# Second pass of a two-block kernel: order of two norms, roots per tile, a projection in two halves, later row fills

## The reference

```python
# end of the first block
h = h + peer(rmsnorm(h, g_ffn[i]), w_q[i], sub_keys[i], expert_u[i], expert_v[i])
gate = jax.nn.sigmoid(rmsnorm(h, g_ple[i]) @ w_pg[i])     # norm n1, product pg
h = h + (p[i] @ w_pe[i]) * gate                           # product e
x = rmsnorm(h, g_final)                                   # norm f
# second block
h = rmsnorm_2(x, g_mix[l])                                # norm n2
proj = h @ w_in[l]                                        # product in2
mixed = concatenate([rmsnorm_2(sb, g_sb_out), rmsnorm_2(pooled, g_pool_out)])
x = x + mixed @ w_out[l]                                  # product o2
x = x + memory_cross_attention(rmsnorm_2(x, g_mem_q), rmsnorm_2(mem, g_mem_kv), ...)   # norm n3, products mq and mo
x = x + moe_ffn(rmsnorm_2(x, g_ffn), ...)                 # norm n4, router, experts
```

## Time and profile before

| | us |
|---|---|
| median of 3 runs | 3245.73 |
| lowest and highest | 3245.32, 3246.43 |
| run of the profiled execution | 3242.78 |
| its span | 3240.9 |
| TensorE busy in the span | 2547.0 (79%) |
| VectorE busy | 1372.6 (42%) |
| ScalarE busy | 682.0 (21%) |
| GpSimd busy | 721.0 (22%) |

### The profile page before, as it was taken

How to read it: one execution, slowest core, us unless ns; L and a number is a source line. 1 busy time by engine, 2 the same in 40 slices (tenths; PEclk the granted TensorE clock), 3 DMA queues, 4 the chain that set the end, 5 groups by cost and what they waited for, 6 DMA issues and landing times. The chain is left out here.

```text
span 3240.9 us, 33257 instructions
## 1 busy us (share of the span) xinstructions
PE 2547.0 (79%) x12781; PEld 1193.5 (37%) x12781; DVE 1372.6 (42%) x3005; ACT 682.0 (21%) x1902; POOL 721.0 (22%) x632
## 2 busy tenths in 40 slices
PE   6987887576556858667687687959999999999994
PEld 3435332242111414322345576723333333333331
DVE  1935667666778686565543123151111111101013
ACT  1112233222223232353231143110000000000001
POOL 0201344334445433644330010200000000000002
PEclk9998998797687979888998899979999999999997
DMA  4217999999999999999996621259999999999997
GB/s 164 78 46 294 407 401 386 372 404 421 421 417 416 418 392 415 378 415 421 421 421 254 194 88 52 69 232 420 406 387 405 412 404 406 413 408 415 404 412 282
DMA packets 152529, 1099.44 MB, mean 339 GB/s; under 512 B 17744, under 2 KB 24400, under 8 KB 54608
## 3 DMA queue, kind: packets, MB, share of 16 engines
q0 software_dynamic: 79232, 556.31, 42.3%
q1 hardware_dynamic: 64848, 529.97, 41.2%
q10 hardware_dynamic: 8288, 11.02, 1.0%
HBM read 1065.77 MB, written 31.46 MB: 339 GB/s over the span
## 5 line engine op out<-in xcount | busy, mean ns | idle before, releaser
L1912 PE MATMUL banks<-arena,spare 128*64 128x512 f32 x2048 | 635.1, 753 | 429.2 <-ACT spare L1853 423.6
L1783 DVE SCALAR_TENSOR_TENSOR arena<-arena 128x1024 f32<-128x1024 f32 x512 | 626.2, 1225 | 446.9 <-DMA arena<-in_expert_uv,picked 446.0
L1674 POOL DMA_INDIRECT arena<-in_expert_uv,picked x512 | 590.2, 1153 | 917.3 <-PE banks L1912 689.0
L2159 PE MATMUL banks<-arena,aT 128*64 128x512 f32 (+1 forms) x4032 | 609.3, 502 | 21.0 <-DMA arena<-in_expert_w 16.1
L1912 PEld LDWEIGHTS banks<-arena,spare 128*64 128x64 f32 x2048 | 147.4, 160 | 836.6 <-ACT spare L1853 607.4
L2159 PEld LDWEIGHTS banks<-arena,aT 128*64 128x64 f32 (+1 forms) x4032 | 208.9, 125 | 395.9 <-issue 341.8
L2171 PE MATMUL banks<-arena,aT 128*64 128x512 f32 (+1 forms) x2016 | 310.8, 509 | 8.9 <-ACT aT L2280 8.7
L2474 DVE TENSOR_SCALAR aT<-banks 128x512 f32<-128x512 f32 (+1 forms) x49 | 30.1, 615 | 632.6 <-PE banks L2177 632.6
L2099 POOL DMA_INDIRECT picked<-moe_rows,extra x32 | 30.5, 954 | 1004.4 <-PE banks L2145 951.7
L1842 ACT ACTIVATE spare<-spare 128x2 f32<-128x2 f32 x256 | 52.0, 203 | 902.3 <-DVE arena L1783 902.0
L1108 PE MATMUL banks<-arena,aT 128*128 128x256 f32 x768 | 179.6, 392 | 1.5 <-DVE aT L1075 0.8
(11 more groups left out here) (303 smaller groups left out, 2096.7 us busy)
## 6 DMA issues: line engine op xcount, KB each, us to landing
arena<-in_expert_w SPq DMA_DIRECT2D x192, 2048.0 KB, 31.9
arena<-in_mid_w SPq DMA_DIRECT2D x58, 1024.0 KB, 9.0
arena<-in_w_q SPq DMA_DIRECT2D x8, 2048.0 KB, 13.9
expert_rows<-aT ACTq DMA_DIRECT2D x70, 128.0 KB, 8.8
arena<-in_expert_uv,picked POOLq DMA_INDIRECT x512, 12.5
expert_rows<-h SPq DMA_DIRECT2D x8, 1024.0 KB, 12.1
arena<-in_w_in SPq DMA_DIRECT2D x3, 2048.0 KB, 19.0
arena<-in_w_out SPq DMA_DIRECT2D x2, 2048.0 KB, 8.2
```

Of the source, the lines that this page charges most:

```text
L1674: eng.indirect_dma_start(places[place_of[n]], None, uv_rows, bass.IndirectOffsetOnAxis(ap=eidx[:, n:n + 1], axis=0))\
L1783: nc.vector.scalar_tensor_tensor(out=u, in0=u, scalar=1.0, in1=twice[tt % 2][:, n % 2, :], op0=ALU.mult, op1=ALU.mult, accum_out=dots[:, k ...
L1912: mm = nc.tensor.matmul(bank[g * HALF:(g + 1) * HALF, sum_bank[tt] + half, :], diag[:, (n + g) % NDIAG, :], places[place_of[n + g]][:, D + ...
L2159: mm = nc.tensor.matmul(bank[tile, b_, 0:width], xT[:, c % 2 * 4 + k, r0:r0 + nrows], w[:, k * D + lo:k * D + lo + width], start=c % 2 == ...
```

## The change

- The first norm of pass two (n1) stands ahead of "mo" of pass one on ScalarE and VectorE, its transposes directly behind "mo" on TensorE. n1 of pass two has row tiles of its own (`rows1[1]`, at region 4096). n4 of pass one stands behind n1's copies on VectorE and its transposes behind pg on TensorE. The wait for the stored rows moves to f's squares.
- In pass two every norm takes root, reciprocal and scaled row one tile after the other.
- In pass two o2 goes over the pooled channels of all four units first (four banks are held), then forms "ssum", then goes over the attention channels.
- The row fills hang on unit ("o2", 1, 3), the router's loads on ("mq", 1, 3).

```diff
             else:
+                pel += [("mo", 0, u) for u in range(4)] + turned_labels("n1", 1) + [("pg", 1, u) for u in range(4)] + turned_labels("n4", 0)
+                acl += squared_labels("n1", 1) + squared_labels("n4", 0)
+                dvl += scaled_labels("n1", 1) + [("mo", 0, u) for u in range(4)] + turned_labels("n1o", 1)
+                dvl += scaled_labels("n4", 0) + turned_labels("n4o", 0)
...
+                if s:
+                    eng.wait_ge(*when("act", (name + "q", s, i)))
+                    nc.scalar.activation(stat[:, c + 2 + i:c + 3 + i], stat[:, c + i:c + i + 1], ACT.Sqrt, scale=1.0 / D,
+                                         bias=const("eps", eps_col, eps_col + 1)).then_inc(mid_act, did("act", (name + "d", s, i)))
...
                 if unit == ("pg", 1, 3):
                     store_rows(0)
                     gains(t["g_final"].rearrange("(o d) -> o d", o=1))
-
+                if unit == ("o2", 1, 3):
                     fills = 0
                     for i in range(OVER_AT, OVER_AT + NBO * 64, W):
                         sp.dma_start(y_dram[i:i + W, :].rearrange("(t p) d -> p t d", p=P), h[:, 0:2, :]).then_inc(rows_filled, 16)
...
-                if unit == ("mo", 1, 3):
+                if unit == ("mq", 1, 3):
                     sp.wait_ge(*when("pe", ("ssum", 1)))
                     sp.wait_ge(*when("pool", ("less", 1, 3)))
                     router_loads(sp)
...
+            if s:
+                eng.wait_ge(*when("dve", ("sn", s, 7)))
+                for ks in (range(4, KD), range(4)):
+                    if ks[0] == 0:
+                        squares("ssum", range(4))
+                        eng.wait_ge(*when("dve", ("sn", s, 3)))
+                    for u in range(4):
+                        unit = ("o2", s, u)
+                        if ks[0]:
+                            eng.wait_ge(unit_in[unit_at[unit][0]], unit_at[unit][1])
+                            begin(eng, unit)
+                        for j in range(2):
+                            for k in ks:
+                                mm = nc.tensor.matmul(bank[:, placed_in[unit], j * W:(j + 1) * W], xT_[s][:, k, j * P:(j + 1) * P],
+                                                      unit_view(unit)[:, k, :], start=k == 4 and j == 0, stop=k == 3, skip_group_check=True)
+                        if ks[0] == 0:
+                            mm.then_inc(mid_pe, did("pe", unit))
...
-            free_rows = [(top, searched[1])] if s == 0 else [(moe_rows_out, 32), when("pe", ("n4", 0, 1, 1))]
+            free_rows = [(top, searched[1])] if s == 0 else []
...
+            stored_rows = [(moe_rows_out, 32)] if s else []
```

## The result

| | before | after |
|---|---|---|
| median, us | 3245.53 (3241.73 to 3246.43) | 3216.96 (3211.19 to 3219.74) |
| profiled execution: run, span | 3242.78, 3240.9 | 3219.14, 3217.3 |

These are medians of four runs each. The ratio is 0.9907, with a 95% interval of 0.9893 to 0.9920: 30 us less, between 26 and 35. The forecast was 33.4 us less and 3212.3 us, with a range of 3206 to 3221.

The account below looks back on a forecast made before the run. One engine works at a time, so TensorE's idle and slow-clock time before the router sets the end of the stretch. 36.0 + 0.8 + 1.1 - 4.5 = 33.4 us off 3245.73 gives 3212.3 us, range 3206 to 3221.

Parts of the forecast that it names:

- n1 ahead of mo, n4 behind pg, fills later: Between mo and e: n1 hidden under mo, n4 computed beside pg, and e's 15.2 us wait for its load gone.
- 3.7 us in place of 18.53: Between the end of mo and the start of pg: TensorE's gap shrinks from 18.53 to 3.7 us.
- Fills at nothing in attention: Row fills moved into pass two's attention: 49.4 us of SyncE's queue taken at no cost, with a bound of 8 us.
- The kinder clock, a rival: in2 and o2's second half escape the slow-clock start, about 2.0 and 1.8 us: 3208.5 us, chance 0.12.
- Router loads: Router loads and the bias split start some 35 us earlier, ahead of pass two's mo, which covers them: nothing.
- Root per tile: Pass two's norms let tile 0 go ahead: 4.1 us saved in f and n2, 0.8 in n3, 1.1 in n4.
- larger switch cost: Table load in f at some 2.66 us, drain included: tile 1's square 0.7 us later, saving 3.4 us, not 4.1.
- o2 in two halves: Pass two's output projection starts earlier, but "ssum" behind the pooled half leaves 4.1 us idle: 4.5 us lost.
- cold start of the second half: o2's second half after the idle gap: a slow-clock start adding 1.8 us to 13.94.
- So what is won before the router moves the whole remainder.: Experts' weight stream starts behind the router and keeps its distance, so all time saved earlier reaches the end.

Follow-up runs that it names:

- the last version: Changed kernel with "ssum" ahead of o2's pooled half, pooled root ahead of the last square, and a constant's root loading the table before the last norm: 3198.54 us, ratio 0.9848.

## Why the prediction was right, and where it was off

The time and the range held: 3216.96 us against 3212.3, in a range of 3206 to 3221. It lies at the upper end of the forecast's own range, 3209 to 3217. Point by point, the forecast's terms against the distances in the table:

- **n1 ahead of mo, n4 behind pg, fills later.** "3.7 us in place of 18.53" was 3.2. The fills alone gave 17.2 us where 15.2 and 2 were forecast. From the end of mo to in2 the forecast was 51.3 us; the trace shows 1812.66 - 1762.12 = 50.5. What the prediction did not say, and the experiments do, is that these two parts can't be added one by one. The fills set the start of "e", so the order without moving them gives next to nothing (110.73, whose gain is the roots' but for 0.2 us), and with them moved 15.4 us (97.96 to 82.59).
- **Fills at nothing in attention.** Right: 137.2 to 137.9 us in six traces with them there, 137.5 and 137.8 in the two of the kernel before. (135.6 us came up twice, once with the fills there and once without; in both traces in2's first four units took 27.89 us, the full clock, for 29.6 to 30.2 in the eight others. That accounts for the 2 us.)
- **The kinder clock, a rival.** It did not come in this trace: in2 began slowly though it now follows 5.9 us of idle and not 10.1 (29.73 us for four units), and so did o2's second half. Two of the other traces with the same 5.93 us of idle have in2 at the full clock, so the rival comes and goes with the execution.
- **Router loads.** Nothing seen: the product behind them ("mo" of pass two) starts with 0.73 us of idle as before. They had no run of their own.
- **Root per tile.** 4.1, 0.8 and 1.1 us were forecast; taking it out cost 4.2, 1.2 and 1.1. The table load took 1.28 us with the next root 0.02 behind, so the larger switch cost of the Trainium skill ("ScalarE: Activation LUTs", What ACT_TABLE_LOAD costs), by which tile 1's square would have been held up, is not what this kernel shows: that square starts at 1804.29, 0.04 us behind the addition that it waits for.
- **o2 in two halves.** The mechanism was right, hole and all: 4.1 us forecast, 4.06 measured. The term for the cold start of the second half was mis-sized. It was taken as 1.8 us, and the half took 16.94 for 13.94: 3.0 us. The clock was at 0.50 for over 4 us behind the hole. So the part lost 5.5 us, not 4.5. The Trainium skill ("TensorE: Matmul & The Clock Gate", What's actually happening) says that the slow clock is the default state and activity releases it. The 0.50 granted after the hole agrees.
- **What the sum held nothing for.** In the profiled execution mq took 2.5 us more at a slow clock, and the other stages up to the slots 1.9 us less. So the 32.5 us of the trace come near the forecast partly by luck. The four parts themselves make 33.1 (36.7, 0.7, 1.2 and -5.5), and the rest, which could have come out some us either way, -0.6.
- **"So what is won before the router moves the whole remainder."** This is the step that did not hold, by 3 to 4 us. The won time arrives at the slots (32.5 us in the profiled execution, against 33.4), but the expert stage behind them took 1100.8 us and not 1097.3. Together with a PEER stage that was 5.4 us longer in that execution, it makes 23.6 of 32.5.

What stays open is why the expert stage is 1.2 to 5.1 us longer in each of the eight traces of changed kernels. Over 820 us of this stage the DMA share is 0.97 to 1.01 in the kernel before, at 391 to 412 GB/s, so its weight stream is what bounds it. Counted from the first issue of an expert weight to the end, it takes 1121.1 and 1121.0 us in the kernel before, 1122.3 with the fills alone moved, and 1123.1 to 1125.6 in the seven traces that hold the changed order and the early router loads. The stage was longer with the fills at their old place (1099.5) and with the fills alone moved (1098.5), with the router stage at 23.8 and at 22.0 us. So neither the place of the fills nor that stage's length sorts them, and no run took the order and the router loads apart.

## What to carry to other kernels

When an engine idles with no releaser named, look at the queue that issues its loads. Here bulk stores with no deadline took 49 us to issue in front of a weight load, and TensorE waited 15 us for it, or 29 us once it arrived earlier. Move them first: the reordering of compute ahead of this queue only lengthened the wait. When a product is split so that half of it starts early, put everything that the second half's chain needs ahead of the first half; 2 us of work left behind it cost 9.

## What had not been expected of the hardware

The same product of 128 instructions takes 27.9 us or up to 30.4 us depending on the clock, and which it is can differ between executions of the same kernel. mq of the changed kernel took 31.05 us to the scores in one trace and 28.59 in the other, though it follows the same 3.3 us of idle and the same 16 transposes. In its first 3 us the granted clock was 0.50 in the one (1.2 GHz) and 1.00 in the other (2.4 GHz). The router's product of the same kernel took 1.95 us in the first trace and 3.59 in the second, and the last product of the memory attention 7.07 and 8.22. A restart after idle cost o2's halves 1.9 us (6.25 us idle) and 3.0 us (4.06 us idle). A gap of 1.44 us (the last version) cost nothing. Differences of this size can't be read from one trace's total.
